# One streaming encoder layer on one core: loads spread over tiles, cached keys turned in head steps, and a reordered SSD

## The chip, the cores and the metric

The kernel runs on one core of a Trainium2 chip. The metric is the device time of one execution in microseconds. Matrix products run on TensorE (PE, with its weight loads shown as PEld), elementwise work on VectorE (DVE), ScalarE (ACT) and GpSimd (POOL); SyncE (SP) and POOL issue most of the DMAs. Products are either fp32, which the trace shows as two instructions each, or fp32r, one instruction each. Where fp32 accuracy is kept with fp32r, a number is split into a high and a low part and the products of the parts are summed.

## What is computed

A layer reads 2048 prompt rows and 64 sample rows of width 1024. The stages after the input projection that matter here, cut from the reference:

```python
# A: attention over the own 64 rows and the 512 before; the sample reads 512 cached keys first
s = einsum('bqhd,bkhd->bhqk', q, concat([k_cache, k_new])) * scale + bias; p = softmax(s); o = p @ v
# B: Mamba-2 SSD in chunks of 128 rows, 6 heads of 64, 2 groups, state 128
acum = cumsum(dt * a)                      # per chunk
decay = exp(where(causal, acum[l] - acum[s], -inf))
y_diag = einsum((c_l . b_s) * decay, x * dt)
st = einsum(b, x * dt * exp(acum[-1] - acum));  h = h * exp(acum[-1]) + st
y = (y_diag + (c . h_prev) * exp(acum) + d_skip * x) * silu(z)
# C: gated MLP, per chunk of 128 and 4 groups:  u * (tril(w) @ v + b)
mixed = concat(rms(o_a), rms(o_b), rms(o_c))
x = layer_norm(alpha * x + mixed @ w_out)
# then up-projection, causal convolution, SwiGLU, down-projection, layer norm
```

Keys of the last 512 prompt rows and of the sample, the final SSD states and convolution states are outputs too.

## The kernel before

Seven stages run one after the other, each a block with a program for every engine and semaphores between them: `project_rows`, `project_features`, `attention`, `ssd_and_gmlp`, `mix_out`, `ffn_up`, `ffn_down`. The order of the work on each engine is written out by hand. Between two stages all engines meet.

`attention` (L916) walks 17 tiles of rows (`Band`), the last being the sample, and in each six heads. One head step on PE (L1238) is `score` of the head after next, `turn` (transposes of the softmax weights, L1214) and `out` of the previous head (L1232). DVE adds the bias (L1091), copies turned blocks (L1119) and normalises (L1106); ACT does the exponential (L1155) and the other turned blocks (L1165). Ahead of tile 14 the loop is left, and `turn_cache` (L1245) turns the 512 cached keys: for each head four transposes into `ps_o` (L1253), a rounded high part by ACT (L1178), the low part by DVE (L1139). Behind the last head, PE turns the keys of five blocks back into rows (L1266, L1267), DVE copies them (L1147), and SP stores them and waits for the stores (L1045). POOL stores the output rows and waits for its stores.

`ssd_and_gmlp` (L1271) begins with DMAs for four constants (`d_row`, `ws`, `gb`, `st_in`, L1350 to L1361), for which PE and POOL wait (`small_loaded`), and with the loads of chunks 0 to 3 (`xbc`, `z`, `uv`, L1355 to L1357). Then 17 chunks run (L1322): 0 to 3 written out, 4 to 11 in a loop, 12 to 16 written out. On PE a step is

```python
front(t + 1)      # 5 transposes into ps_r; 6 fp32 products with `upper` (cumulative sums) into ps_a; 2 products into ps_c
state products into ps_st; products with the state into ps_off; 6 into ps_diag; 4 gate products into ps_c (L1640)
```

On DVE a step copies two small vectors (L1492, L1493), forms the differences of sums from `ps_a` (six operations, L1504), masks `ps_c` (L1508), then `y1` (L1537), the new state (L1539), the mixing matrix of the next chunk (L1518), `y3` (L1545) and the gated output `oc` (four operations, L1551). ACT copies the turned rows (L1446) and takes the exponential (L1448). POOL scales (L1407 to L1409), decays the state (L1416), adds the skip (L1419) and gates with `z` (L1423, `ob`). SP stores `oc` and `ob` and then loads chunk t+4 into the slot of chunk t. Ahead of the loop SP issues the eight loads of `w_out` in one go (L1381) and one of `g_mix`. From chunk 12 on ACT rounds two of the eight `w_out` blocks per step (L1461).

`mix_out` (L1668) walks 17 tiles of rows: 48 products with `w_out` (L119 to L121), transposes of the next tile's `mx` (L1994) and of the last tile's result (L2002), and on DVE scaling, sum and layer norm, of which L1941 writes the result. SP loads `mx` and `x` two tiles ahead (L1753, L1760). Ahead of tile 8 SP also issues, in one go, the loads of the first unit of `ffn_w_in` (L1779) and four blocks of the transposed result (L1783 to L1786), which ACT and DVE prepare for `ffn_up` in tiles 9 to 13.

## Time and profile before

| what | value |
|---|---|
| time, median of 3 runs | 2712.58 us (2704.79 to 2712.89) |
| time of the profiled execution | 2708.32 us |
| its span, first to last instruction | 2706.9 us |
| mean granted TensorE clock | 0.976 |
| PE busy | 2554.4 us, 94% of the span |
| PEld busy | 2349.3 us, 87% |
| DVE busy | 1636.4 us, 60% |
| ACT busy | 1052.8 us, 39% |
| POOL busy | 190.1 us, 7% |
| attention, first to last product | 609 to 839 us |
| SSD and gated MLP | 845 to 983 us |
| mixing | 986 to 1226 us |

A busy share is a mean over stages with different limits. A row of the timeline gives the start in us, the duration in us, the engine, the line, the operation, output and inputs, how many it stands for, and in brackets the idle time of the engine before it with what ended that. SPq is the DMA queue of SP: its rows are issues.

### The profile page before, as it was taken

To read this page: it belongs to the slowest core of one execution; us is meant where nothing else is said; L and a number is where in the kernel's file an instruction comes from. 1 tells how busy PE (TensorE), PEld (TensorE's weight loads), DVE (VectorE), ACT (ScalarE), POOL (GpSimd) and SP (SyncE) were. 2 spreads that over 40 slices of the span, in tenths; PEclk is the share of its full clock that TensorE was granted. 3 is DMA by queue.
4 is the path that set the end of the run, shared out by engine and by line. 5 is a ranking of instruction groups with operands and counts; after the bars stand their busy time and mean duration, and the time that the engine had idled before them with its cause. 6 is when DMAs were issued, how large, how long until landed. Compare 5 with 4: busy or idle time off the path is not lost. (4 is left out here: it accounts for less than half of the span.)

```text
span 2706.9 us, 46923 instructions
## 1 busy us (share of the span) xinstructions
PE 2554.4 (94%) x15072; PEld 2349.3 (87%) x15072; DVE 1636.4 (60%) x3300; ACT 1052.8 (39%) x2000; POOL 190.1 (7%) x276
## 2 busy tenths in 40 slices
PE   6999899989997889897999999999999999999998
PEld 5888799989987878777999989999999978888885
DVE  5433455457775776677999966668666653333332
ACT  4454422226552232225555544445555451111110
POOL 0001100011002641010000000000000000000000
PEclk9999999999998989999999999999999999999999
DMA  6446434236543734548777788887888753223221
GB/s 195 152 139 200 159 108 158 78 102 155 123 98 116 237 131 156 198 140 262 232 253 243 248 286 262 258 256 233 257 256 254 247 187 119 80 80 94 79 79 52
DMA packets 407770, 471.10 MB, mean 174 GB/s; under 512 B 40074, under 2 KB 340732, under 8 KB 407650
## 3 DMA queue, kind: packets, MB, share of 16 engines
q1 hardware_dynamic: 388722, 409.13, 48.4%
q0 software_dynamic: 18944, 60.64, 7.0%
q8 instruction: 58, 0.95, 0.2%
q14 instruction: 46, 0.38, 0.0%
HBM read 315.00 MB, written 157.57 MB: 175 GB/s over the span
## 5 line engine op out<-in xcount | busy, mean ns | idle before, releaser
L2612 PE MATMUL fu_ps_a<-mo_fu_x_hi,mo_fu_w 128*128 128x354 f32 (+1 forms) x1056 | 347.1, 329 | 23.6 <-DVE fu_c L2575 9.6
L2614 PE MATMUL fu_ps_a<-mo_fu_x_hi,mo_fu_w 128*128 128x354 f32 (+1 forms) x1056 | 344.4, 326 | 0.0
L119 PE MATMUL fd_ps_y<-fu_fd_w,fu_fd_h_hi 128*128 128x512 f32 (+1 forms) x748 | 292.4, 391 | 6.7 <-PEq L2043 6.1
L120 PE MATMUL fd_ps_y<-fu_fd_w,fu_fd_h_hi 128*128 128x512 f32 (+1 forms) x748 | 291.7, 390 | 0.0
L121 PE MATMUL fd_ps_y<-fu_fd_w,fu_fd_h_lo 128*128 128x512 f32 (+1 forms) x748 | 291.5, 390 | 0.0
L2803 DVE TENSOR_TENSOR fu_fd_h_lo<-fu_fd_h_raw,fu_fd_h_hi 128x256 fp32r<-128x256 f32 (+1 forms) x185 | 76.9, 416 | 308.9 <-ACT fu_fd_h_hi L2773 308.8
L2613 PE MATMUL fu_ps_a<-fu_x_lo_rest,mo_fu_w 128*128 128x354 f32 (+1 forms) x792 | 257.3, 325 | 0.0
L2773 ACT CAST fu_fd_h_hi<-fu_fd_h_raw 128x256 fp32r<-128x256 f32 (+1 forms) x185 | 74.0, 401 | 403.2 <-PE fd_ps_y L121 396.4
L2612 PEld LDWEIGHTS fu_ps_a<-mo_fu_x_hi,mo_fu_w 128*128 128x128 f32 x1056 | 200.4, 190 | 31.6 <-DVE mo_fu_w L2485 10.9
L2614 PEld LDWEIGHTS fu_ps_a<-mo_fu_x_hi,mo_fu_w 128*128 128x128 f32 x1056 | 200.1, 189 | 0.0
L2612 PE MATMUL fu_ps_c<-mo_fu_x_hi,mo_fu_w 128*128 128x354 f32 (+1 forms) x528 | 173.2, 328 | 8.7 <-ACT fu_part L2407 8.7
L119 PEld LDWEIGHTS fd_ps_y<-fu_fd_w,fu_fd_h_hi 128*128 128x128 f32 (+1 forms) x748 | 138.4, 185 | 40.2 <-issue 6.4
L2613 PE MATMUL fu_ps_c<-fu_x_lo_rest,mo_fu_w 128*128 128x354 f32 (+1 forms) x528 | 172.9, 327 | 0.0
L2614 PE MATMUL fu_ps_c<-mo_fu_x_hi,mo_fu_w 128*128 128x354 f32 (+1 forms) x528 | 172.4, 327 | 0.0
L121 PEld LDWEIGHTS fd_ps_y<-fu_fd_w,fu_fd_h_lo 128*128 128x128 f32 (+1 forms) x748 | 138.4, 185 | 32.0
L120 PEld LDWEIGHTS fd_ps_y<-fu_fd_w,fu_fd_h_hi 128*128 128x128 f32 (+1 forms) x748 | 138.5, 185 | 31.4
L119 PE MATMUL pr_ps_y<-pr_w_hi,pr_xt_hi 128*128 128x512 f32 (+3 forms) x408 | 148.6, 364 | 4.7 <-DVE pr_xt_lo L382 4.7
L2613 PEld LDWEIGHTS fu_ps_a<-fu_x_lo_rest,mo_fu_w 128*128 128x128 f32 x792 | 149.9, 189 | 0.0
L120 PE MATMUL pr_ps_y<-pr_w_lo,pr_xt_hi 128*128 128x512 f32 (+3 forms) x408 | 147.8, 362 | 0.0
L121 PE MATMUL pr_ps_y<-pr_w_hi,pr_xt_lo 128*128 128x512 f32 (+3 forms) x408 | 147.0, 360 | 0.0
L2353 ACT ACTIVATE fu_gate<-fu_c,fu_vecs 128x352 f32<-128x352 f32 (+1 forms) x132 | 90.1, 682 | 85.0 <-DVE fu_c L2556 69.1
L119 PE MATMUL mo_ps_y<-sg_mo_w_hi,sg_mo_mt_hi 128*128 128x512 f32 (+1 forms) x272 | 109.2, 401 | 6.1 <-POOL mo_ident L127 6.1
(396 smaller groups left out, 6239.2 us busy)
## 6 DMA issues: line engine op xcount, KB each, us to landing
mo_fu_w<-fu_w_split SPq DMA_DIRECT2D x176, 512.0 KB, 4.4
fu_w_raw<-ffn_w_in SPq DMA_DIRECT2D x131, 512.0 KB, 5.7
fu_w_split<-mo_fu_w SPq DMA_DIRECT2D x44, 1024.0 KB, 5.9
fu_fd_h_raw<-h_t SPq DMA_DIRECT2D x176, 128.0 KB, 2.2
h_t<-fu_val SPq DMA_DIRECT2D x88, 176.0 KB, 1.9
fu_fd_raw<-ffn_w_out SPq DMA_DIRECT2D x22, 512.0 KB, 4.4
x_rows<-pr_xr SPq DMA_DIRECT2D x16, 512.0 KB, 2.8
xt<-pr_xt SPq DMA_DIRECT2D x16, 512.0 KB, 4.0
```

The source lines that it names most:

```text
L119: pe.matmul(out, lhs_hi, rhs_hi, start=first, stop=False)
L120: pe.matmul(out, lhs_hi, rhs_lo, start=False, stop=False)
L121: return pe.matmul(out, lhs_lo, rhs_hi, start=False, stop=last)
L2353: act.activation(out, src[:, 0:n], ACT.Identity, bias=one(vecs[:, 3, :], mt), scale=one(vecs[:, 0, :], mt)).then_inc(tap0_done, 1)
L2612: pe.matmul(out, wh, xh, start=first and k == 0, stop=False, skip_group_check=True)
L2613: pe.matmul(out, wh, xl, start=False, stop=False, skip_group_check=True)
L2614: last = pe.matmul(out, wl, xh, start=False, stop=k == KH - 1, skip_group_check=True)
L2773: act.copy(h_hi[:, x.slot, :, :x.n], h_raw[:, x.slot, :, :x.n]).then_inc(h_hi_done, 1)
L2803: dve.tensor_tensor(h_lo[:, x.slot, :, :x.n], h_raw[:, x.slot, :, :x.n], h_hi[:, x.slot, :, :x.n].bitcast(F32), ALU.subtract).then_inc(h_l ...
```

## The change

- Attention: two of the four blocks of a head's cached keys are turned in each of the twelve head steps of tiles 14 and 15; four of the five blocks of keys are turned back inside the last two head steps. POOL issues the loads of SSD chunks 0 and 1 at the beginning of tiles 14 and 15 and of the four constants at tile 16. SP and POOL no longer wait for the stores at the end; SP does so at the end of the SSD stage.
- SSD: chunks 0 and 1 are read where attention put them; SP loads 2 to 5 at the beginning. The two small copies move from DVE to ACT, and so do the differences, as `Relu` with a scale of -1 ahead of the exponential. The sums are made from a high and a low part in fp32r. PE does the gate products of chunk t in `front(t + 1)`, behind the sums, and DVE writes `oc` right behind the mask. POOL decays the state first and gates chunk t-1 behind the scaling of t+1. `oc` and `ob` have semaphores of their own. `w_out` is loaded block by block, behind the stores of chunks 0 to 3 and of chunks 4, 6, 8 and 10.
- Mixing: the loads for `ffn_up` are spread over tiles 8 to 12, between the `mx` and the `x` load of a tile, and the work on them moves to tiles 10 to 15.

```diff
 attention, PE and POOL
+                    if turns_cache(b):
+                        turn_cache(b, h)
...
+                def turn_cache(b, h):
+                    i, n = turn_of(b, h), HEADS * b.t + h
+                    if i == 0:
+                        pe.wait_ge(cache_loaded, 16 * 8)
+                    pe.wait_ge(o_done, n - 1)
+                    for k in range(2):
+                        twice = cache[:, 2 * (i % 2) + k, i // 2].rearrange("p a f -> p (a f)")
+                        last = pe.transpose(ps_o[:, i % 2, k * P:(k + 1) * P], twice, ident[:])
...
+                    if turns_cache(b):                       # out()
+                        pe.wait_ge(cache_lo_done, turn_of(b, h) + 1)
...
-                sp.wait_ge(rows_stored, 32)
...
+                pool.wait_ge(next_loaded, 16 * 10)
 SSD, SP
+                for t in range(2, 6):
+                    load(t, t % 4)
...
-                    if not isinstance(t, int) or t + 4 <= NT:
+                    if not isinstance(t, int) or 2 <= t and t + 4 <= NT:
                         load(t + 4, b)
+                    if isinstance(t, int) and t < 4:
+                        sp.dma_start(mo["w_raw"][:, t, :], d["w_out"][t * P:(t + 1) * P, :]).then_inc(mo["w_loaded"], 16)
+                    if not isinstance(t, int) and b % 2 == 0:
+                        k = 2 * i + 2 + b // 2
+                        sp.dma_start(mo["w_raw"][:, bass.ds(k, 1), :], d["w_out"][bass.ds(k * P, P), :]...).then_inc(mo["w_loaded"], 16)
 SSD, POOL
                 def step(t, b, p, i):
+                    decay(t)
                     if not isinstance(t, int) or t + 1 <= NT:
                         scale(t + 1, 1 - p)
-                    back(t, b, p, i)
+                    if not (isinstance(t, int) and t == 0):
+                        gate(t - 1, (b - 1) % 4, 1 - p, i if b else i - 1)
+                    add_own(t, p)
 SSD, ACT
+                    for h in range(HEADS):
+                        last = act.activation(seg[:n, p, h, :n], ps_a[:n, h * P:h * P + n], ACT.Relu, bias=cum_t[:n, p, h:h + 1], scale=-1.0)
+                    last.then_inc(seg_done, 1)
                     act.wait_ge(seg_done, t + 1)
-                    act.activation(seg[:n, p, :, :n], seg[:n, p, :, :n], ACT.Exp).then_inc(exp_done, 1)
+                    act.activation(seg[:n, p, :, :n], seg[:n, p, :, :n], ACT.Exp, scale=-1.0).then_inc(exp_done, 1)
...
                     if 12 <= t < NT:
+                        act.wait_ge(mo["w_loaded"], 16 * KD)
                         for k in (2 * (t - 12), 2 * (t - 12) + 1):
-                            act.wait_ge(mo["w_loaded"][k], 16)
 SSD, PE
                     for h in range(HEADS):
-                        last = pe.matmul(ps_a[:n, h * P:h * P + n], dta_t[:n, p, h:h + 1].to_broadcast([n, n]), upper[:n, :n],
-                                         start=True, stop=True)
+                        for e in range(2):
+                            steps = dta_t[:n, p, e * HEADS + h:e * HEADS + h + 1].to_broadcast([n, n])
+                            last = pe.matmul(ps_a[:n, h * P:h * P + n], steps, upper_r[:n, :n], start=e == 0, stop=e == 1)
                     last.then_inc(cum_done, 1)
                     wait_if(pe, cbm_done, t)
                     wait_if(pe, oc_done, t - 1)
+                    if not (isinstance(t, int) and t == 0):
+                        gates(t - 1, (b - 1) % 4)
 mixing, SP
+                    if isinstance(t, int) and t >= 8:
+                        load_next(t)             # between load_mx(t + 2) and load_x(t + 2)
...
+                    if t == 8:                   # the two halves of unit_raw
+                    if t == 9:                   # X_T1
+                    if t == 10:                  # X_B22
+                    if t == 11:                  # X_B11
+                    if t == 12:                  # X_B21
```

## Rows read from the trace of the kernel before

**Rows 1.** Timeline (columns as told above) of the cached keys' turn, 783 to 791 us.

```profile
783.44 1.06 PE L1253 MATMUL at_ps_o<-at_ident,at_cache 128*128 128x128 f32 x8 [0.67 <-DVE at_o L1106]
...
787.02 0.69 DVE L1139 TENSOR_TENSOR pf_at_k<-at_ps_o,pf_at_k 128x512 fp32r<-128x512 f32 x1 [1.01 <-ACT pf_at_k L1178]
...
790.91 0.49 PE L1199 MATMUL at_ps_s<-pf_at_k,pf_at_q 128*128 128x512 f32 x1 [1.40 <-DVE pf_at_k L1139]
```

**Rows 2.** Timeline from the last head to the first SSD product, 830 to 853 us.

```profile
830.36 0.19 PEld L1266 LDWEIGHTS at_ps_s<-at_ident_r,pf_at_k 128*128 128x128 f32 x1
...
836.64 0.33 PEld L1267 LDWEIGHTS at_ps_s<-at_ident_r,pf_at_k 128*128 128x128 f32 x1
...
840.29 0.52 SPq L1044 DMA_DIRECT2D sample_k<-at_k_rows  x1
844.81 0.21 POOL L125 MEMSET sg_ident<- 128x128 f32 x1 [12.75 <-POOLq L919]
...
853.04 1.09 PE L1588 MATMUL sg_ps_off<-sg_ident,sg_ws 128*128 128x128 f32 x4 [13.79 <-DMA sg_st_in<-state_ssm]
```

**Rows 3.** Timeline of PE's weight loads in one SSD chunk, 867 to 875 us.

```profile
867.70 0.52 PEld L1607 LDWEIGHTS sg_ps_c<-sg_xbc 128*128 128x128 f32 x4 [0.91 <-issue]
...
872.17 1.42 PEld L1601 LDWEIGHTS sg_ps_a<-sg_upper,sg_dta_t 128*128 128x128 f32 x12
...
874.23 0.52 PEld L1607 LDWEIGHTS sg_ps_c<-sg_xbc 128*128 128x128 f32 x4 [0.64 <-issue]
```

**Rows 4.** Busy time by stretch: start:end, length, then each engine, PEclk, DMA share, GB/s.

```profile
880.57:893.60 13.03, 12.11 (x98) 11.79 (x98) 11.63 (x37) 3.07 (x4) 10.08 (x13) 1.00 0.67 195
906.60:919.70 13.10, 8.63 (x56) 8.63 (x57) 5.68 (x18) 1.53 (x2) 5.17 (x6) 0.74 0.81 275
```

**Rows 5.** Timeline of the chunk loads and of w_out's, 866 to 912 us.

```profile
866.89 0.99 POOL L1423 TENSOR_TENSOR sg_ob<-sg_y,sg_z 128x384 f32<-128x384 f32 x1 [1.43 <-DVE sg_y L1545]
...
869.85 0.43 SPq L1357 DMA_DIRECT2D sg_uv<-uv_rows  x1
...
892.59 3.35 SPq L1381 DMA_DIRECT2D sg_mo_w_raw<-w_out  x5
...
911.07 0.93 PEld L1596 LDWEIGHTS sg_ps_r<-sg_ident,sg_xbc 128*128 128x128 f32 x5 [6.58 <-DMA sg_uv<-uv_rows]
```

**Rows 6.** Timeline of the mixing's layer norm on DVE, 1097 to 1164 us, and PE's stall.

```profile
1097.64 1.28 DVE L1941 SCALAR_TENSOR_TENSOR mo_y<-mo_y,mo_rs,mo_b_ln 128x1024 f32<-128x1024 f32 x1
...
1117.17 1.97 PE L1994 MATMUL mo_ps_m<-mo_ident,sg_mo_mx 128*128 128x128 f32 x8 [10.93 <-DVE sg_mo_mx L1890]
...
1135.54 1.29 DVE L1941 SCALAR_TENSOR_TENSOR mo_y<-mo_y,mo_rs,mo_b_ln 128x1024 f32<-128x1024 f32 x1
1148.22 1.28 DVE L1941 SCALAR_TENSOR_TENSOR mo_y<-mo_y,mo_rs,mo_b_ln 128x1024 f32<-128x1024 f32 x1
...
1162.07 1.63 DVE L1974 TENSOR_TENSOR mo_fu_xb<-mo_fu_xb 128x1416 f32<-128x1416 f32 x1
```

**Rows 7.** Timeline of an ordinary head step, 769 us.

```profile
769.30 0.53 PEld L1214 LDWEIGHTS at_ps_t<-at_ident,at_s 128*128 128x128 f32 x5
...
769.74 0.83 DVE L1091 CUSTOM_DVE_ANT_0 at_s<-at_ps_s,pf_bias 128x640 f32<-128x640 f32 x1 [0.41 <-PE at_ps_s L1200]
```

**Rows 8.** DMA issues, 867 to 885 us: count, KB each, us to landing.

```profile
sg_xbc<-xbc_t SPq DMA_DIRECT2D x3, 448.0 KB, 4.3
```

**Rows 9.** Groups by line, 880 to 945 us: busy us, mean ns, idle before, releaser.

```profile
L1504 DVE TENSOR_SCALAR sg_seg<-sg_ps_a,sg_ncum_t 128x128 f32<-128x128 f32 x54 | 14.7, 336 | 5.3 <-PE sg_ps_a L1601 5.3
...
L1448 ACT ACTIVATE sg_seg<-sg_seg 128x768 f32<-128x768 f32 x9 | 7.6, 844 | 26.6 <-DVE sg_seg L1504 26.6
...
L1446 ACT COPY sg_rows<-sg_ps_r 128x640 f32<-128x640 f32 x8 | 5.5, 692 | 24.1 <-PE sg_ps_r L1596 24.1
...
L1461 ACT CAST sg_mo_w_hi<-sg_mo_w_raw 128x1024 fp32r<-128x1024 f32 x2 | 2.0, 1035 | 0.0
```

**Rows 10.** Timeline of ACT in the last chunk: a table load.

```profile
972.06 1.28 ACT L1474 ACT_TABLE_LOAD   x1
```

More of the change, by code:

```diff
@@ L1335, in chunks, with in_place, slot @@
                 step(t, t % 4, t % 2, t // 4)
+        def in_place(t):
+            return isinstance(t, int) and t < 2
+        def slot(name, t, b):
+            if in_place(t):
+                return head[name][:, t]
+            return {"xbc": xbc_slots, "z": z_slots, "uv": uv_slots}[name][:, b]
         def col(t):
@@ L1624, in step @@
                     wait_if(pe, y1_done, t)
[L1625 to L1626 removed]
                     for g in range(2):
                         c = slice(3 * g * HD, 3 * (g + 1) * HD)
[L1629 removed]
+                        last = pe.matmul(ps_off[:n, c], slot("xbc", t, b)[:, 5 + g, :n], state[:, c], start=True, stop=True)
                     last.then_inc(off_done, 1)
```

339 lines of the change are left out of this document (197 added, 142 removed).

## The prediction

> **What bounds the kernel now.** I read the page first, then the busy times by stretch, the waits, the timeline of each place that the diff touches, and the DMA issues. PE is busy for 94% of the span, so a gain must come from a stretch in which PE stands idle or runs at the lower clock. The change touches three stages, 609 to 1226 us, and they hold five such places. (1) Ahead of tile 14 PE turns cached keys alone: its ordinary work stops until 790.91 [rows 1]. (2) From the last head at 830.36 to the first SSD product at 853.04 PE has only keys to turn back and then waits 13.79 us, at the end for the constant `st_in` [rows 2]. (3) In the SSD a chunk takes 6.53 us from one pair of `ps_c` products to the next, and just ahead of them PE's loads stand idle for 0.64 us [rows 3]: these products wait for `oc`, the last thing that DVE does in a step. DVE is busy for 11.63 of 13.03 us, POOL for 10.08, ACT for 3.07 [rows 4]: DVE's order sets the period and ACT is free. (4) `w_out`'s burst at 892.59 delays a chunk's loads, and PE's loads stand idle 6.58 us [rows 5]; the granted clock of that stretch is 0.74 [rows 4]. (5) In the mixing PE stands idle 10.93 us [rows 6] behind the burst of six loads for the next stage. The reader is to see in each group which engine's row ends the idle time in brackets.
>
> **Cached keys.** Removed: PE's turn starts at 783.44 after 0.67 us of idle, and scores resume at 790.91, so 790.91 - 783.44 + 0.67 = 8.1 us. Added: 24 transposes in 12 head steps. Five transposes take 0.53 us in a head step [rows 7], in which PE's loads have next to no idle, so two add 0.21 and the twelve steps 2.5 us. DVE has 0.41 us of idle in a step [rows 7] and gets a subtraction of half the size of L1139's 0.69 us [rows 1], 0.35 to 0.45 us: it fills up, and `out` now waits for it. That may cost up to another 0.2 us a step. I take 0.3 in all, 3.6 us; bounds 2.5 and 5.5. Gain 4.5 us (2.6 to 5.6).
>
> **End of attention.** PE still makes the 60 products behind the keys, 48 of them ahead of the last two `out`; as PE is full there, this moves work and removes none. I take 1.5 us (0 to 2.9). The wait for the stores: SP's last issue ends at 840.81 and the next stage begins at 844.81 [rows 2]; the two ends of a stage without such a wait are not in these rows, so I bound the gain by 0 and 2 us and take 1.3. POOL's new wait is for loads issued tiles earlier; behind it nothing is queued but the end of the stage. The ten loads of 2.3 MB for chunks and constants run beside heads whose own loads are few; I cost them at nothing, and if that cover is gone, a head waits as long as one such load lands, 4.3 us [rows 8].
>
> **Start of the SSD.** PE began 853.04 - 844.81 = 8.2 us into the stage. Afterwards it waits only for POOL's masks, four short operations that start with the one of 0.21 us at 844.81 [rows 2]: some 1.2 us. Gain 7.0 us (6 to 7.3). ACT must first split the steps and round `upper`, six short copies in a chain with DVE; they lie beside PE's nine transposes.
>
> **The chunk's period.** PE's own work is 6.53 - 0.64 = 5.9 us [rows 3]. The twelve fp32 instructions of the sums take 1.42 us [rows 3], 0.12 each; the twelve in fp32r that replace them are bounded, as an estimate, by 0.11 us for a load of 0.19 us that overlaps its neighbour [rows 2] and 0.14: 1.3 to 1.7 us, and I keep 1.4. Now the walk through one step of 5.9 us from PE's first transpose: sums end at 2.1, gates 2.9, `ps_c` pair 3.4, `ps_off` 4.6, `ps_diag` 6.0. ACT: rows at 0.9 for 0.69, six `Relu` (bound by the DVE form's 1.6 us for six below and 0.3 each above) from 2.1 to 3.9, exponential 0.84, small copies 0.4: 3.8 of 5.9 us [rows 9]. DVE loses the differences and copies, 1.6 + 0.6 us of its 5.8 per chunk: mask, `oc`, `y1`, state, mixing, `y3` end at 7.5, long before the next mask at 9.4. POOL has 5.2 us: scaling to 3.9, the gate to 4.9, then it waits for `y1` at 5.3 and ends at 6.4, still ahead of the next rows. So PE becomes the bound at 5.9 us and nothing else has less than half a us of slack. Gain 0.64 x 15 periods = 9.6 us. Bounds: 6.2 us a chunk (5.0 us gained) and 5.75 (11.7).
>
> A rule of the Trainium skill speaks against moving the differences: ScalarE: Activation LUTs, section on rules for kernel authors, sends `relu` to VectorE and not to ScalarE. The row gives DVE 0.34 us for one of 128 columns [rows 9], no run here yet has ACT's; by that rule alone the six would rather cost some tenths more, which matters only where ACT is full.
>
> **The loads.** `w_out` no longer comes in a burst. PE's 6.58 us go, and so does the low clock behind them, at which five transposes took 0.93 us [rows 5] and not 0.53 as in [rows 7], and the rest of a chunk likewise: about 1 us. Together 7.5 us gained (5 to 8). But two new waits come. First, SP loads chunk t+4 behind `ob` of chunk t, which POOL now makes a step later. POOL's gate ends at 867.88 and the last of the three loads is issued by 870.28 [rows 5], and a load lands in 4.3 us [rows 8]: 4.9 + 2.4 + 4.3 = 11.6 in the step's time, and PE wants it at 2 x 5.9 = 11.8. Nearly no slack; a rival below. Second, ACT waits ahead of chunk 12 for all eight blocks of `w_out`, and the last is issued only in SP's step 10, behind `ob` of chunk 10, thus in PE's step 11 at 7.3, landing at 11.6, that is 5.7 in step 12. ACT is there at 4.7 of step 11, and behind its wait stand two roundings of 1.035 us [rows 9], rows, `Relu` and exponential of chunk 13. PE's transposes of chunk 14 need these rows at 8.9 instead of 5.9, its sums the `Relu` at 10.5 instead of 6.5: 4.1 us lost, and one more if the clock falls. I take -5 (-7 to 0). SSD's tail: `oc` and gates earlier, DVE relieved: 1.5 us (0 to 3).
>
> **Mixing.** Two tiles took 1135.54 - 1097.64 = 37.9 us where one takes 1148.22 - 1135.54 = 12.7 [rows 6]: 12.5 us lost to the burst. Spread, a tile carries at most 1 MB more beside its 2 MB in 12.7 us, about 240 GB/s, less than the 275 GB/s of a stretch above [rows 4]. The `mx` load stands ahead of the added one in each tile. DVE gets two block operations of 1.63 us [rows 6] in tiles 13 and 14 each, 3.3 us on about 2.4 of idle: it falls 1.8 us behind, while PE wants its low parts 6 us later, and it has made that good by tile 16. Gain 12.5 us (7 to 12.6).
>
> **Sum.** 4.5 + 1.5 + 1.3 + 7.0 + 9.6 + 7.5 - 5 + 1.5 + 12.5 = 40.4 us. Against the profiled execution, 2708.3 us (span 2706.9), that is 2667.9; the three runs' median is 4.3 us above that execution and their lowest 3.5 below, so I leave the forecast at 2668.
>
> **The rivals.** (A) Chunk loads late: each step's loads land after PE wants them. For: the slack of 0.2 us above, and `w_out` and 0.3 MB of stores in the same queue. Against: `xbc` is issued first of the three, and loads overlap. Each us late costs half a us a period, as a slot's cycle spans two steps; at 1.3 us late the period is back at 6.5 and 9.6 us are gone: 2677. (B) `Relu` and the exponential need different tables: two table loads a chunk, 1.28 us each as the one for the square root behind the last chunk [rows 10]. ACT: 3.8 + 2.6 = 6.4 us, and 8.4 in the four chunks with roundings: 0.5 x 12 + 2.5 x 4 = 16 us, 2684. Against: copies and exponentials alternate here without one [rows 9]. The Trainium skill, ScalarE: Activation LUTs, section on table sets, has `relu` in every set, by which this rival would be void; no row has the pair. (C) The slower one: the clock stays at 1.2 GHz in the SSD, because fp32r sums keep the array less busy than fp32 ones. The place where it fell, 830 to 837 us, is one of pure fp32r with 64 columns [rows 2]; here they are 1.4 of 5.9 us, between fp32 groups at full clock [rows 4]. Price: the lower clock stretches a chunk to some 10.5 us, 4.6 x 16 = 74 us on top: 2742. It decides from nine chunks at the low clock on. (D) ACT's wait for `w_out` costs nothing, since the block lands early or ACT runs behind: 2663. (E) The spreading in the mixing does not do what it says: each of four added loads still holds the next `mx` for some 2 us past its slack, 8 us: 2676.
>
> **How the numbers follow.** Forecast as summed 0.55, A 0.13, B 0.04, C 0.04, D 0.14, E 0.10. All but C are faster by over 0.3% (8 us, about what a measurement of this kernel can tell from no change). The best ends of all bounds together give 2655, the worst without a rival 2690; I take 2656 to 2684, which holds D, A, E and B's middle. Faster 0.94, within 0.3% 0.02, slower 0.04.
>
> **What would show it.** Right: no L1253 alone on PE; head steps in tiles 14 and 15 longer by 0.3 us; PE's first SSD product 1.2 us into the stage; `ps_c` pairs 5.9 us apart with no idle ahead of them; one idle stretch of PE of 3 to 4 us at chunk 13 with ACT's cast ending it on a DMA; mixing tiles 12.7 us apart throughout. Wrong: PE's transposes idle on `sg_uv`, table loads in the SSD, or a granted clock under 0.9 from chunk 2 on.

## The result

The changed kernel takes 2684.32 us (median of four runs, 2679.94 to 2686.66) against 2711.05 us (2704.79 to 2712.89) for the kernel before: ratio 0.9905, interval 0.9888 to 0.9921. It is faster by 26.7 us, where 40.4 were forecast against the profiled execution (43 against this median), and it lies 0.3 us above the range. The two profiled executions differ by less, 2706.9 - 2685.2 = 21.7 us of span, and the places below add up to that.

The page of the changed kernel gives the busy time by engine: PE is busy as long as before, ACT 33 us longer, POOL 15 us longer, and DVE only 16 us less.

```profile
span 2685.2 us, 46989 instructions
PE 2555.4 (95%) x15072; PEld 2352.2 (88%) x15072; DVE 1620.2 (60%) x3171; ACT 1086.0 (40%) x2144; POOL 204.7 (8%) x286
```

**Attention.** These lines are the timeline of a head step in tile 14, which answers to [rows 1] and [rows 7]. The two transposes of cached keys stand behind the turn, ACT and DVE split them within the step, and a step takes 787.05 - 784.51 = 2.54 us, where it took 2.33 before. PE no longer turns cached keys alone.

```profile
784.51 0.73 PE L1262 MATMUL at_ps_t<-at_ident,at_s 128*128 128x128 f32 x5
785.08 0.38 PE L1311 MATMUL at_ps_o<-at_ident,at_cache 128*128 128x128 f32 x2
785.50 0.37 ACT L1224 CAST pf_at_k<-at_ps_o 128x256 fp32r<-128x256 f32 x1
786.97 0.41 DVE L1178 TENSOR_TENSOR pf_at_k<-at_ps_o,pf_at_k 128x256 fp32r<-128x256 f32 x1
787.05 0.74 PE L1262 MATMUL at_ps_t<-at_ident,at_s 128*128 128x128 f32 x5
```

**The end of attention and the start of the SSD.** This is PE's timeline, answering to [rows 2]. The products that turn the keys back begin at 822.39 at full clock (0.28 us each); from 825.32 on they take 0.36 to 0.40 us, and the last heads' own products stand behind them: the 20 products of the last `out` take 2.97 us, where they took 1.80 before. The wait for the next stage is 5.55 us and not 13.79.

```profile
822.39 0.30 PE L1326 MATMUL at_ps_s<-at_ident_r,pf_at_k 128*128 128x64 f32 x1
...
825.21 0.28 PE L1326 MATMUL at_ps_s<-at_ident_r,pf_at_k 128*128 128x64 f32 x1
825.32 0.36 PE L1327 MATMUL at_ps_s<-at_ident_r,pf_at_k 128*128 128x64 f32 x1
825.49 0.40 PE L1326 MATMUL at_ps_s<-at_ident_r,pf_at_k 128*128 128x64 f32 x1
...
830.19 0.79 PE L1262 MATMUL at_ps_t<-at_ident,at_s 64*128 64x64 f32 x5
...
833.61 2.97 PE L1282 MATMUL at_ps_o<-pf_at_v,at_pt 128*64 128x64 f32 x20
...
843.54 1.11 PE L1684 MATMUL sg_ps_off<-sg_ident,at_sg_ws 128*128 128x128 f32 x4 [5.55 <-POOL sg_upper L1479]
```

The busy time by stretch behind that product (columns as in [rows 4]) shows PE busy without a break, while the granted clock stays at 0.50, the 1.2 GHz level, until 859 us.

```profile
845.00:850.00 5.00, 5.00 (x25) 4.81 (x24) 0.81 (x2) 2.45 (x8) 3.19 (x4) 0.50 1.05 323
850.00:855.00 5.00, 5.00 (x24) 5.00 (x24) 1.03 (x2) 3.64 (x11) 2.46 (x3) 0.50 1.09 328
855.00:859.00 4.00, 4.00 (x17) 4.00 (x16) 2.12 (x7) 0.57 (x3) 0.29 (x1) 0.50 0.19 69
859.00:861.00 2.00, 2.00 (x18) 2.00 (x18) 2.00 (x3) 0.33 (x1) 1.81 (x2) 0.87 0.00 0
```

**The chunks.** An undisturbed chunk takes 5.82 us, 6.53 before [rows 3]. The timeline of PE's weight loads shows every idle time of over 0.5 us between the first product and the sums of chunk 16, and what ended it. The first four are waits for chunk loads (one is put down to "issue"; the run with early loads below removes it with the others). The 4.00 us in step 13, ahead of the transposes of chunk 14, are ACT's wait for `w_out`, whose row stands in the second fence beside the issue of the last block: ACT had been idle 8.25 us.

```profile
884.60 0.53 PEld L1703 LDWEIGHTS sg_ps_r<-sg_ident,sg_xbc 128*128 128x128 f32 x5 [1.38 <-DMA sg_uv<-uv_rows]
896.91 0.53 PEld L1703 LDWEIGHTS sg_ps_r<-sg_ident,sg_xbc 128*128 128x128 f32 x5 [0.60 <-DMA sg_uv<-uv_rows]
904.31 0.53 PEld L1703 LDWEIGHTS sg_ps_r<-sg_ident,sg_xbc 128*128 128x128 f32 x5 [1.49 <-issue]
922.49 0.53 PEld L1703 LDWEIGHTS sg_ps_r<-sg_ident,sg_xbc 128*128 128x128 f32 x5 [0.65 <-DMA sg_uv<-uv_rows]
938.26 0.93 PEld L1703 LDWEIGHTS sg_ps_r<-sg_ident,sg_xbc 128*128 128x128 f32 x5 [4.00 <-issue]
939.83 2.63 PEld L1712 LDWEIGHTS sg_ps_a<-sg_upper_r,sg_dta_t 128*128 128x128 f32 x12 [0.63 <-issue]
```

```profile
930.48 0.35 SPq L1454 DMA_DIRECT2D sg_mo_w_raw<-w_out  x1
935.37 1.99 ACT L1575 CAST sg_mo_w_hi<-sg_mo_w_raw 128x1024 fp32r<-128x1024 f32 x2 [8.25 <-DMA sg_mo_w_raw<-w_out]
```

The `uv` load is the last of the three that a chunk needs. The four that PE waited for took 6.0, 4.9, 5.9 and 4.7 us from issue to landing. Here is the first, as the list of DMA issues shows it (count, KB each, us to landing):

```profile
sg_uv<-uv_rows SPq DMA_DIRECT2D x1, 256.0 KB, 6.0
```

**The mixing.** DVE's timeline, answering to [rows 6], has 12.65, 12.84 and 12.48 us from tile to tile where the burst stood.

```profile
1087.07 1.28 DVE L2056 SCALAR_TENSOR_TENSOR mo_y<-mo_y,mo_rs,mo_b_ln 128x1024 f32<-128x1024 f32 x1
1099.72 1.28 DVE L2056 SCALAR_TENSOR_TENSOR mo_y<-mo_y,mo_rs,mo_b_ln 128x1024 f32<-128x1024 f32 x1
1112.56 1.28 DVE L2056 SCALAR_TENSOR_TENSOR mo_y<-mo_y,mo_rs,mo_b_ln 128x1024 f32<-128x1024 f32 x1
1125.04 1.28 DVE L2056 SCALAR_TENSOR_TENSOR mo_y<-mo_y,mo_rs,mo_b_ln 128x1024 f32<-128x1024 f32 x1
```

**Where 21.7 us came from.** The table goes by landmarks in the two timelines: the first score, the turn of the sample's fourth head, the end of the keys, the stage's first product, the sums of chunks 2 and 16, the first and the last layer norm of the mixing. A period is the time from one chunk's sums to the next chunk's.

| place | before, us | changed, us | gain | forecast |
|---|---|---|---|---|
| first score to the fourth head (cached keys) | 216.5 | 211.0 | 5.5 | 4.5 |
| fourth head to the last key | 13.7 | 16.9 | -3.2 | 1.5 |
| last key to the first SSD product | 13.8 | 5.55 | 8.25 | 8.3 |
| first product to the sums of chunk 2 | 12.4 | 16.9 | -4.4 | 0 |
| period, 14 chunks: 6.53 and 5.82 | 91.4 | 81.5 | 9.9 | 9.6 |
| over the period: burst before; late loads and ACT's wait after | 8.2 | 13.8 | -5.6 | 7.5 - 5 |
| sums of chunk 16 to the first layer norm of the mixing | 42.77 | 43.14 | -0.4 | 1.5 |
| first to last layer norm | 215.6 | 201.4 | 14.2 | 12.5 |
| ahead of attention and behind the mixing, untouched code | | | -2.6 | 0 |

The 13.8 us are the sum of what the intervals between the sums have over 5.82: 1.45 + 0.68 + 1.57 + 0.72 = 4.4 for loads, 5.15 for ACT's wait, 4.03 for the chunk behind it at the low clock, 0.2 for the rest. Three places, then, take back most of what was forecast: the keys among the heads, the low clock at the start of the SSD, and the waits inside it. Of the mixing's 14.2 us, 12.4 lie in the two tiles of the burst (37.9 and 25.5 us) and 1.6 in the first tile (13.84 and 12.27 us from the first layer norm to the second). A second profile of the changed kernel has 13.87 us there, so these 1.6 us do not come from the change. The untouched code behind the last layer norm takes 1481 to 1486 us over all profiles, so the last row lies within the spread of code that nobody changed.

### The profile page after: what moved, and what is told of

The parts are those of the page before. It is cut to its first block and busy times, and to the rows that moved or that the text cites. A ratio compares the mean times of both kernels' runs of the same rounds, so it can differ in the third digit from the quotient of the medians.

```text
span 2685.2 us, 46989 instructions
## 1 busy us (share of the span) xinstructions
PE 2555.4 (95%) x15072; PEld 2352.2 (88%) x15072; DVE 1620.2 (60%) x3171; ACT 1086.0 (40%) x2144; POOL 204.7 (8%) x286
```

## The experiments

Each is the changed kernel with one edit, if nothing else is said. Where a kernel was run once, its time is given for orientation only, and the verdict rests on the profile. One profile of the chunks is a weak base as well: the same code took 95.3, 98.4, 97.8 and 102.9 us from the sums of chunk 2 to those of chunk 16 in four profiles (the changed kernel, the keys last, the burst in the mixing, and the changed kernel again).

**Keys behind the last head.**

```diff
                     if nxt2:
                         score(nxt2)
-                    if last_heads:
-                        turn_keys(2 * (h - HEADS + 2))
                     turn(cur)
-                    if last_heads:
-                        turn_keys(2 * (h - HEADS + 2) + 1)
                     if prev:
                         out(prev)
...
                 out((Band(NT), 0, HEADS - 1))
-                turn_keys(4)
+                for b in range(5):
+                    turn_keys(b)
```

> The changed kernel, but all five blocks of keys are turned back behind the last head, as before the change. In the changed kernel PE needs 16.8 us from the turn of the sample's fourth head (821.09 us) to the end of the keys (837.9 us), and the kernel before needed 13.3 us for the same work. My theory: blocks 0 to 3 inside the last two heads bring the clock down early, at 825.3 us, and the last head's own work then runs at 1.2 GHz. It expects 13.3 us here, thus 3.5 us less. Rival: the keys cost the same wherever they stand; it expects 16.5 to 17 us. A second question in the same run: PE's clock stays at 1.2 GHz for 15.7 us of work after the SSD's first product. If that comes from the long low stretch before, it should fall to 4 to 6 us here; if it comes from the SSD's own products, it stays 15 to 16 us.

Measured: 2682.86 us. From the fourth head's turn (820.86) to the last key (833.60) it took 12.7 us, against 16.9 in the changed kernel and 13.7 before. The busy time by stretch shows that the clock holds through all heads and falls at 830.

```profile
826.00:828.00 2.00, 2.00 (x20) 2.00 (x19) 0.81 (x2) 0.00 (x0) 0.57 (x1) 1.00 0.02 5
828.00:830.00 2.00, 2.00 (x19) 2.00 (x19) 0.64 (x2) 0.00 (x0) 0.00 (x0) 0.97 0.21 45
830.00:832.00 2.00, 2.00 (x11) 2.00 (x11) 0.47 (x1) 0.00 (x0) 0.00 (x0) 0.50 0.00 0
```

Over all profiles of this study that stretch took 15.3 to 17.4 us with the keys among the heads (11 profiles) and 12.0 to 14.6 with the keys last (5). The cost of the new place is shown. It is larger than this stretch says: the wait that follows is 4.10 us here and 5.55 in the changed kernel, and it is so in every other profile of either order but the one with wide products; why is not shown. The second question is answered too: the sums of chunk 2 still came 16.89 us after the first product, so the early fall is not what keeps the clock down in the SSD. The whole time hardly fell, as late loads and the low clock behind them made the chunks 3 us longer than in the changed kernel's profile.

**Sums in fp32.**

```diff
-                        for e in range(2):
-                            steps = dta_t[:n, p, e * HEADS + h:e * HEADS + h + 1].to_broadcast([n, n])
-                            last = pe.matmul(ps_a[:n, h * P:h * P + n], steps, upper_r[:n, :n], start=e == 0, stop=e == 1)
+                        last = pe.matmul(ps_a[:n, h * P:h * P + n], dta_t[:n, p, h:h + 1].to_broadcast([n, n]), upper[:n, :n],
+                                         start=True, stop=True)
```

> The changed kernel, but with the twelve instructions of the cumulative sums as six fp32 products again instead of twelve fp32r ones. My theory: the fp32r sums with their broadcast left side hold the clock at 1.2 GHz once it is low, so the clock needs 15.7 us of work to come back at the start of the SSD and 10 us behind the stall at 938 us, where the kernel before needed 4.2 and 4.6 us. It expects 4 to 8 us of low clock at the start here, the sums of chunk 2 at 12 to 14 us after the first product instead of 16.85, and 4 to 5 us less in all with what comes back behind the stall. Rival: the low clock comes from the short idle stretch and the keys before it; then the start stays at 15 to 16 us. Both expect the period of an undisturbed chunk to stay within 0.1 of 5.82 us, since the twelve instructions take 1.42 us either way.

Measured: 2681.02 us. The twelve instructions take 2.69 us for chunk 0 and 1.41 for chunk 1, as the weight loads show; in the changed kernel both took over 2.6. The sums of chunk 2 come at 12.47 us. Behind the stall that ends at 930.63 the clock is back by 936.0, after 5.4 us; in the changed kernel it took from 938.3 to 948, 10 us. The two intervals at that stall are hardly shorter for it, 10.35 and 10.23 us against 10.96 and 9.85, as a second stall lies in the latter. The period stayed 5.82.

```profile
843.19 2.69 PEld L1710 LDWEIGHTS sg_ps_a<-sg_upper,sg_dta_t 128*128 128x128 f32 x12
847.98 1.41 PEld L1710 LDWEIGHTS sg_ps_a<-sg_upper,sg_dta_t 128*128 128x128 f32 x12 [0.44 <-issue]
853.80 1.42 PEld L1710 LDWEIGHTS sg_ps_a<-sg_upper,sg_dta_t 128*128 128x128 f32 x12
```

That second stall is the load of chunk 15, late by 2.43 us, and from the sums of chunk 2 to those of chunk 16 it took 96.1 us, no less than 95.3. Two later runs showed an early return with fp32r, so that this one alone does not settle the cause; see the four timed runs below.

**Two semaphores for `w_out`.**

```diff
                     if isinstance(t, int) and t < 4:
-                        sp.dma_start(mo["w_raw"][:, t, :], d["w_out"][t * P:(t + 1) * P, :]).then_inc(mo["w_loaded"], 16)
+                        sp.dma_start(mo["w_raw"][:, t, :], d["w_out"][t * P:(t + 1) * P, :]).then_inc(mo["w_first"], 16)
...
-                        act.wait_ge(mo["w_loaded"], 16 * KD)
+                        act.wait_ge(mo["w_first"] if t < 14 else mo["w_loaded"], 16 * 4)
```

> The changed kernel, but the first four blocks of w_out signal a semaphore of their own, so that ACT waits ahead of chunks 12 and 13 for these alone, and for the last four ahead of chunk 14. My theory: the wait for all eight blocks costs the 5.15 us of the stall that ends at 938 us and the 4.0 us of low clock behind it, 9.2 us together; it expects chunk intervals of 5.8 to 6.6 us throughout from chunk 2 on and some 9 us less. Rival: ACT is full in the chunks with roundings (two of 1.0 us on top of 3.4 of 5.82 us) and DVE too, so that half of it stays: 4 to 5 us less. A second rival: the other chunk loads collide with the w_out block all the same and the stall moves to the load of chunk 14.

Measured: 2679.07 us. Nothing waits in step 13: the interval to the sums of chunk 14 is 5.83. But the load of chunk 15 is then late, the second rival in part, and with the clock falling it costs 7.59 and 9.27 us for two intervals.

```profile
938.02 0.53 PEld L1703 LDWEIGHTS sg_ps_r<-sg_ident,sg_xbc 128*128 128x128 f32 x5 [1.70 <-DMA sg_uv<-uv_rows]
```

From the sums of chunk 2 to those of chunk 16 it took 89.8 us, 5.5 less than 95.3 and not the 9 expected. That the wait of 4.00 us came from the count is shown by its absence; how much it cost in all is known only within the spread told above.

**Early loads.**

```diff
                     sp.dma_start(d["mixed"][tile_rows(t), 2 * AW:], oc[:n, p, :]).then_inc(oc_stored[p], 16)
+                    if again:
+                        sp.wait_ge(off_done, t + 1)
+                        load(t + 4, b, ("xbc", "uv"))
                     sp.wait_ge(ob_done, t + 1)
...
-                        load(t + 4, b)
+                        load(t + 4, b, ("z",))
```

`z` has semaphores of its own, for which POOL's gate waits.

> The changed kernel, but SP loads xbc and uv of chunk t+4 as soon as the products with the state and oc of chunk t are done, some 5 us earlier; z comes behind ob as before, with a semaphore of its own for which POOL waits and not PE. My theory: PE's four waits for chunk loads (1.38, 0.60, 1.49 and 0.65 us, 4.1 us in all) come from the late issue; it expects none over 0.2 us, and 4 us less. Rival: they come from the bandwidth, since the DMA queues are busy at a share of 0.98 to 1.00 from 884 to 896 us while w_out blocks are in flight; then at least half of the 4.1 us stay, at the same places.

Measured: 2680.07 us, and every interval from chunk 2 to chunk 13 is 5.82 us: no wait for a load is left, so the earlier issue cures the lateness. The busy time by stretch where `w_out` is in flight shows that the queues are as full as in the changed kernel (0.99, 317 GB/s) and move more, so a full queue by itself did not make a load late.

```profile
884.00:896.00 12.00, 12.00 (x103) 12.00 (x103) 9.98 (x22) 6.87 (x21) 11.83 (x13) 1.00 1.04 346
```

What is left is ACT's wait, with 2.24 us of idle ahead of chunk 14 and intervals of 9.20 and 9.10. That the queue's load played no part is not shown: of the four late `uv` loads of the changed kernel each landed 0.4 to 1.7 us later than the 4.3 us that the prediction took, about as much as PE waited.

**Differences on DVE again.** The six operations stand ahead of DVE's mask:

```diff
 ACT
-                        last = act.activation(seg[:n, p, h, :n], ps_a[:n, h * P:h * P + n], ACT.Relu, bias=cum_t[:n, p, h:h + 1], scale=-1.0)
 DVE
+                        last = dve.tensor_scalar(seg[:n, p, h, :n], ps_a[:n, h * P:h * P + n], cum_t[:n, p, h:h + 1], 0.0,
+                                                 ALU.subtract, ALU.min)
```

> The changed kernel, but the six differences per chunk are formed on DVE again (subtraction and minimum with zero) ahead of the mask, and ACT takes only the exponential; the new place of oc and of the gate products stays. In the changed kernel DVE is busy for 4.99 of a 6.0 us stretch, its mixing operations lengthened to 1.15 us each from 0.73. My theory: with 1.6 to 2.0 us more DVE has some 6.6 us per chunk and sets the period again, so undisturbed chunks take 6.3 to 6.7 us in place of 5.82, and the run is 7 to 12 us slower than the changed kernel. Rival: the period fell because oc and the gate products moved, and DVE's work has slack; then it stays at 5.82 to 5.95 us.

Measured: 2681.76 us and 5.82 us a chunk: the rival was right for the differences. DVE has no idle time at all (the third busy figure below), and PE still none. The two small copies, some 0.6 us a chunk on DVE before, stayed on ACT in this run; as DVE is full, it does not show that they could go back as well.

```profile
866.00:872.00 6.00, 6.00 (x53) 6.00 (x53) 6.00 (x16) 1.91 (x5) 5.57 (x7) 1.00 0.56 149
```

**The burst in the mixing.** The conditions for tiles 9 to 12 go, so that all six loads are issued at tile 8.

```diff
+                    if isinstance(t, int) and t == 8:
+                        load_next(t)
                     if exists(t, 2):
                         load_mx(t + 2, p)
-                    if isinstance(t, int) and t >= 8:
-                        load_next(t)
...
-                    if t == 9:
...
-                    if t == 10:
```

> The changed kernel, but the six loads for the next stage stand in one go at tile 8 of the mixing, ahead of its mx load, as before the change; the work on them stays in tiles 10 to 15. My theory: the burst alone makes the 12.5 us lost in two tiles before; it expects the layer norms of tiles 8 to 10 to be 24 and 13.7 us apart again, and the mixing 12 to 13 us longer than the 201.4 us of the changed kernel. Rival: part of the gain of 14.2 us is the later work on DVE and ACT; then it is 6 to 10 us longer only.

Measured: 2699.6 us, and DVE's timeline shows the gap of before, with 25.07 and 14.96 us for two tiles.

```profile
1086.56 1.28 DVE L2052 SCALAR_TENSOR_TENSOR mo_y<-mo_y,mo_rs,mo_b_ln 128x1024 f32<-128x1024 f32 x1
1111.63 1.29 DVE L2052 SCALAR_TENSOR_TENSOR mo_y<-mo_y,mo_rs,mo_b_ln 128x1024 f32<-128x1024 f32 x1
1126.59 1.28 DVE L2052 SCALAR_TENSOR_TENSOR mo_y<-mo_y,mo_rs,mo_b_ln 128x1024 f32<-128x1024 f32 x1
```

From the first to the last layer norm it took 216.0 us against 201.4, 14.6 more and not the 12 to 13 expected. The spread loads are thus all of the gain, and the later work on DVE and ACT gave none.

**All four edits at once.** These are the first four diffs together.

> The changed kernel with four edits at once: keys turned back behind the last head, sums in fp32, two semaphores for the blocks of w_out, and the early loads of xbc and uv. My theory: the stall ahead of chunk 13 and the four waits for loads go (13.8 us over the 81.5 us of 14 undisturbed periods), the end of attention gives 4.2 us and the start of the SSD 4.4 us, so the sums of the last chunk come 94 to 97 us after the first product in place of 112.2, and the time is 2662 us (2657 to 2667), 0.982 of the kernel before. Rival: with the stalls gone the w_out blocks and the chunk loads collide in chunks 13 to 15, where the split of w_out and two more loads of mx stand; then 5 us of it stay, 2667 to 2671 us.

Measured: 2658.9 us (2658.03 to 2660.07), ratio 0.9816 (0.9802 to 0.9829). From the sums of chunk 2 on all intervals are 5.82 us, but for the last with 5.91; the sums of chunk 16 come 94.04 us after the first product, where 94 to 97 were expected, and the time is within its 2657 to 2667 too. PE's weight loads show no idle time over 0.2 us between chunk 1 and chunk 16.

```profile
842.40 1.41 PEld L1711 LDWEIGHTS sg_ps_a<-sg_upper,sg_dta_t 128*128 128x128 f32 x12 [0.74 <-issue]
929.89 0.77 PEld L1711 LDWEIGHTS sg_ps_a<-sg_upper,sg_dta_t 64*64 64x64 f32 x12 [0.20 <-issue]
```

**Wide products in the gap.** They come on top of the four edits:

```diff
+                for k in range(5):
+                    pe.matmul(ps_t[:, 512:1024], keys(0, 0, 12), kr[:, 12, 0:512], start=True, stop=True)
...
+                for k in range(2):
+                    pe.matmul(ps_diag[:, 0:256], ws[:, 0, :], ws[:, 0:2, :].rearrange("p g j -> p (g j)"), start=True, stop=True)
```

> The kernel with the four edits, and in the gap between the two stages PE does five wide fp32r products of 512 columns behind the keys and two fp32 products of 256 columns ahead of the wait for the masks; nobody reads them. My theory: they are PE work in a gap, so the clock, low from 829.9 us on in the run with the keys last, comes back by the first chunk's sums instead of some 4 to 6 us after the first product; 1.5 to 2 us less up to the sums of chunk 2. Rival: five products at the low clock take 2.1 us and the clock counts from the stage's start all the same, since there is still an idle wait of 2 us between; no gain, or up to 1 us lost.

Measured: 2662.01 us. The clock was back for the first sums (1.42 us for twelve), but from the last key to the sums of chunk 2 it took 15.84 us, against 16.0 to 16.6 in the three runs with the keys last and an early return. That is 0.1 us below the lowest of them, where 1.5 to 2 us less were expected, so no gain is shown.

**`oc` last.** It stands behind `y3` again.

```diff
                         causal(t + 1, 1 - p)
-                    dve.wait_ge(gm_done, t + 1)
-                    for g in range(CG):
...
                     dve.tensor_tensor(y3[:n, :], y2[:n, :], ps_diag[:n, 0:AW], ALU.add).then_inc(y3_done, 1)
+                    dve.wait_ge(gm_done, t + 1)
+                    for g in range(CG):
```

> The changed kernel, but DVE writes oc behind y3, as the last thing of its step, as before the change; the differences stay on ACT and the gate products stay in PE's next step. The run with the differences back on DVE kept the period of 5.82 us, with DVE busy for 6.00 of 6.00 us, so the move to ACT is not what shortened it. Theory: it was the place of oc. With oc last, PE's products into ps_c wait for it again: but DVE has 1.66 us less in its step here, so oc ends at about 8.4 us counted from PE's first transpose and is wanted at 8.7; it expects a period of 5.82 to 6.0 us. Rival: either edit alone is enough, as each takes 1 to 2 us out of the time from the sums to oc; it expects 5.82 exactly.

Measured: 2707.62 us, a period of 7.45, and both expectations are far off. PE's weight loads stand idle ahead of the gate products in every step, from the third on for 1.0 to 1.9 us.

```profile
868.06 0.97 PEld L1692 LDWEIGHTS sg_ps_c<-sg_uv,sg_wt 128*128 128x128 f32 x8 [1.55 <-issue]
```

`oc` ran at 867.09 to 867.94, behind `y3` and the two mixing operations, which took 2.22 us together. I had DVE's walk end at 8.4 us with mixing operations of 0.73 us.

**Both undone.** This is the last diff and that of the differences together.

> The changed kernel with both edits undone at once: the differences on DVE and oc behind y3 (the gate products stay in PE's next step, POOL's order stays). If the new place of oc or the move to ACT, either one, gave the period, it is back at 6.4 to 6.8 us here and PE's loads stand idle ahead of the products into ps_c. If it was neither, but the gate products or POOL's new order, it stays at 5.82 to 5.9 us.

Measured: 2708.6 us, with intervals of 7.2 to 7.5 us and 9.1 to 9.3 in several; 6.4 to 6.8 were expected. The differences add nothing here either. In the changed order the place of `oc` decides between 7.45 and 5.82 us a chunk. That is more than the gain of 0.71 over the kernel before, so the rest of the new order costs time while `oc` is last; what the gate products, POOL's order and the moved copies give by themselves was not separated.

**`w_out` in one go again.** The loads block by block go, and the eight stand ahead of chunk 4.

```diff
-                    if isinstance(t, int) and t < 4:
-                        sp.dma_start(mo["w_raw"][:, t, :], d["w_out"][t * P:(t + 1) * P, :]).then_inc(mo["w_loaded"], 16)
...
                     if t == 4:
+                        for k in range(KD):
+                            sp.dma_start(mo["w_raw"][:, k, :], d["w_out"][k * P:(k + 1) * P, :]).then_inc(mo["w_loaded"], 16)
```

> The changed kernel, but the eight loads of w_out come in one go ahead of chunk 4, as before the change, with the one semaphore for which ACT waits ahead of chunk 12. Theory: the burst stalls PE for 6 to 8 us once, with 5 to 10 us of low clock behind it, since the sums are fp32r; in return the stall of 5.15 us ahead of chunk 13, its 4.0 us of low clock and the waits for single loads behind chunk 7 go. It expects the sums of the last chunk 110 to 115 us after the first product against 112.2 in the changed kernel: the spreading gave nothing net as it was done. Rival: the spreading is worth its 7.5 us, the burst costs more than the late wait, and the chunks take 117 us or more.

Measured: 2687.66 us. The burst cost 10.26 us of idle and a chunk at the low clock, two intervals of 16.62 and 10.33; behind it the intervals were 5.82 or 5.83, 6.06 and 6.88. The sums of chunk 16 came 110.9 us after the first product, inside the theory's 110 to 115. But the start was quick here (chunk 2's sums at 12.29), so I compare from there: 98.6 us to chunk 16, against 95.3 in the one profile of the changed kernel and 102.9 in the other. That the spreading as it was done is worth anything net is not shown.

```profile
899.57 0.93 PEld L1699 LDWEIGHTS sg_ps_r<-sg_ident,sg_xbc 128*128 128x128 f32 x5 [10.26 <-DMA sg_uv<-uv_rows]
900.49 2.68 PEld L1708 LDWEIGHTS sg_ps_a<-sg_upper_r,sg_dta_t 128*128 128x128 f32 x12
```

**Four timed runs on one chip.** They are the changed kernel, the same with fp32 sums, with the other three edits, and with all four.

> The changed kernel itself, as the base for the next three on the same chip. Expected 2680 to 2687 us, and a profile in which the sums of chunk 2 come 16 to 17 us after the stage's first product, or, where the clock returns early as it did in one run of nine, 12.3 us.

> The changed kernel with fp32 sums, timed. If the type of the sums delays the clock's return, the median is 3 to 6 us below that of the changed kernel on the same chip, and the sums of chunk 2 come 12.3 to 12.5 us after the first product again. If the three early returns were chance, the medians agree within 1.5 us and the profile may show either.

> The kernel with three of the four edits (keys last, two semaphores, early loads), the sums left in fp32r. If the sums cost what they seem to, it is 3 to 6 us above the kernel with all four, thus 2662 to 2665 us, with 16 to 17 us from the first product to the sums of chunk 2. If not, it is at 2658 to 2660 us like the kernel with all four.

> The kernel with all four edits again, on the same chip as the three before. Expected 2657 to 2661 us and the sums of chunk 2 12.3 to 12.6 us after the first product; any other interval there would speak against the sums as the cause.

| kernel | median, us | lowest to highest | ratio to before (interval) | sums of chunk 2 after the first product |
|---|---|---|---|---|
| changed | 2685.44 | 2679.86 to 2692.27 | 0.9903 (0.9885 to 0.9922) | 16.74 us |
| fp32 sums | 2679.94 | 2678.55 to 2680.45 | 0.9885 (0.9867 to 0.9903) | 12.48 |
| three edits, fp32r sums | 2659.97 | 2658.92 to 2661.33 | 0.9813 (0.9798 to 0.9829) | 11.86 |
| four edits, fp32 sums | 2660.08 | 2657.11 to 2660.68 | 0.9812 (0.9797 to 0.9827) | 12.17 |

In the changed kernel the median is 5.5 us lower with fp32 sums, though the lowest of its runs, 2679.86 us, lies within theirs, and their spread is 1.9 us against 12.4. Beside the other three edits they give nothing: the run with three edits met the expectation for sums that do not cost (2658 to 2660 us), and the early sums of chunk 2 in the last run, 12.17 us, lie outside the 12.3 to 12.6 that I had tied to the sums as the cause. The profiled run of the changed kernel, its slowest with 2692.27 us, shows what the spread is made of: a load late by 2.55 us, and the chunk behind it takes 894.66 - 885.55 = 9.11 us and not 5.82, since the clock fell.

```profile
885.06 0.53 PEld L1703 LDWEIGHTS sg_ps_r<-sg_ident,sg_xbc 128*128 128x128 f32 x5 [2.55 <-DMA sg_uv<-uv_rows]
885.55 2.28 PEld L1712 LDWEIGHTS sg_ps_a<-sg_upper_r,sg_dta_t 128*128 128x128 f32 x12
894.66 1.42 PEld L1712 LDWEIGHTS sg_ps_a<-sg_upper_r,sg_dta_t 128*128 128x128 f32 x12
```

With fp32 sums a late load, of 1.68 us, made intervals of 8.09 and 6.87. At the start of the SSD the clock came back late in 9 of 11 profiles with fp32r sums (chunk 2's sums at 15.2 to 16.9 us) and early in 2 (12.29 and 11.86), and early in 5 of 5 with fp32 sums (the kernel before counted, the run with wide products not). So the sums' type goes with the delay but does not fix it alone: with fp32r sums and the keys last, the sums of chunk 2 came at 16.89 us in one kernel and at 11.86 in another whose PE code up to there is the same. Why those two came back early stays open, and with it what delays the clock in the others.

## Why the prediction was wrong

The sign and six of the nine terms held in size: cached keys (4.5 forecast, 5.5 measured), the start of the SSD with the wait for stores (8.3 and 8.25), the period (9.6 and 9.9), the burst (7.5 and 8.2), the mixing (12.5 and 14.2, of which 12.4 in the tiles of the burst). The gain stayed out in the places that follow.

- **End of attention: forecast +1.5, measured -3.2.** The failed step is "mixed with fp32 work the fall may come later or not at all". I priced the low clock for the keys alone. It fell about as far into the keys, 3.0 us against 3.2 before, and as the keys now stand ahead of the last heads' work, that work ran at 1.2 GHz too. The run with the keys last gives it back.
- **Start of the SSD: forecast 0, measured -4.4.** The failed step is a missing term: I took the gap as the whole cost and did not ask at which clock the stage starts. Rival C came nearest, fp32r sums that hold the clock down, but it had them lower the clock for the whole stage, at 74 us. In undisturbed chunks the clock is full with either kind of sums; the delay shows where it is already low, at the start. That fp32r sums cause it is not shown, as two of eleven profiles with them had none.
- **ACT's wait: forecast 5, measured 9.2** (5.15 and 4.03). The place and the cause were right, the idle of PE too, "3 to 4 us" against 4.00. Mis-sized was the clock, "one more if the clock falls": 9.2 less the 4.1 of the wait leaves 5 us, because the clock took 10 us to return, more than a chunk and a half.
- **Late chunk loads: forecast 0, with rival A at 0.13.** The walk gave 0.2 us of slack, and four loads were late, 4.4 us with what follows, more in the run of 2692.27 us. The failed step is "a load lands in 4.3 us", a row of `xbc` ahead of `w_out`'s burst: the last load of a chunk is `uv`, and the four late ones took 4.7 to 6.0 us. The early loads show that an issue ahead of `ob` gives slack enough for that.
- **Tail of the SSD: forecast +1.5, measured -0.4.** From the sums of chunk 16 to the first layer norm of the mixing it took 42.8 us before and 43.1 in the changed kernel, so the term "`oc` and gates earlier, DVE relieved" gave nothing. No run looked into it, and the cause stays open.
- **The period was right in part by luck.** The step "DVE loses the differences" has no part in it: with the differences back the period is the same. It is `oc` ahead of the state work, worth 1.6 us in the new order. The durations were wrong as well: a mixing operation takes 1.15 us and not 0.73, and POOL's decay 1.15 and not 0.83, as the groups of the changed kernel show.

```profile
L1619 DVE TENSOR_TENSOR sg_mix<-sg_seg,sg_cbm 128x384 f32<-128x384 f32 x20 | 22.2, 1147 | 0.0
L1498 POOL TENSOR_TENSOR sg_decayed<-sg_state,dt_etot 128x384 f32<-128x384 f32 x10 | 11.5, 1146 | 0.0
```

The Trainium skill, GPSIMD Engine Reference, section on specifications, says that the engine shares its SBUF interfaces with VectorE, with contention for DVE instructions that have two SBUF inputs. These mixing operations have two, and the rows agree. They show more: the two engines take turns. In the timeline of the changed kernel a mixing operation ends 0.41 us after the POOL operation that it started beside (872.52 and 872.11; 873.63 and 873.21), and POOL's decay, started in between, ends 0.69 us after the mixing operation. The kernel before has the same 0.41 us (872.41 and 872.00); where POOL was idle, a mixing operation took 0.55 us.

```profile
871.11 1.00 POOL L1511 TENSOR_TENSOR sg_y<-sg_y,sg_xd 128x384 f32<-128x384 f32 x1
871.41 1.11 DVE L1619 TENSOR_TENSOR sg_mix<-sg_seg,sg_cbm 128x384 f32<-128x384 f32 x1
872.07 1.14 POOL L1498 TENSOR_TENSOR sg_decayed<-sg_state,dt_etot 128x384 f32<-128x384 f32 x1
872.45 1.18 DVE L1619 TENSOR_TENSOR sg_mix<-sg_seg,sg_cbm 128x384 f32<-128x384 f32 x1
...
865.81 0.55 DVE L1518 TENSOR_TENSOR sg_mix<-sg_seg,sg_cbm 128x384 f32<-128x384 f32 x1
871.54 0.87 DVE L1518 TENSOR_TENSOR sg_mix<-sg_seg,sg_cbm 128x384 f32<-128x384 f32 x1
```

The last two lines are from the kernel before. All mixing operations together took 23.8 us before and 37.3 in the changed kernel. That is one reason why moving 2.2 us a chunk away lowered DVE's busy time by so little, and it made the expectation for `oc` last fail.

Rival B is void: the only table load of the stage stands at 961.68 us, in the last chunk as before [rows 10]. Six `Relu` take 1.66 us on ACT, as many differences 1.63 on DVE. The rule on `relu` of the Trainium skill, ScalarE: Activation LUTs, section on rules for kernel authors, is thus neither confirmed nor costly here: at 128 columns of fp32 both engines need about 0.28 us each. Rival D fell, and so did E: where the loads are spread, the tiles of the mixing are 12.5 to 12.8 us apart.

The range missed by 0.3 us for the median and by 1.4 us for that of the later five runs. Its upper end held the cases one by one, but late loads, the clock at the start, the cost of the keys and a longer wait came together. That it missed by so little is luck: the profiled executions differ by 21.7 us, not 26.7, and the mixing and the cached keys gave 2.7 us more than forecast.

## What to carry to other kernels

Price a stall together with the clock behind it: here 2 to 4 us of idle cost 3 to 5 us more at 1.2 GHz, while the waits of 0.6 to 1.5 us in the changed kernel left the clock at 1.00 and cost little more than themselves. A load with 0.2 us of slack is thus worth moving even where it looks just in time. Take the landing time from the row of the load that comes last, and from a stretch with the same traffic. Don't put a run of narrow products ahead of real work, but behind the last of it. When loads are counted on one semaphore, ask at which count each waiter could go on; and when an order changes, find by undoing one move at a time which of the moves pays, since here `oc` ahead of the state work decided the period and moving the differences off DVE gave nothing. Compare profiles of the same code before you read 3 us out of one profile.

## What the runs showed of the hardware

- In the changed kernel PE was busy without a break at a granted clock of 0.50 for 15.5 us, from 843.5 to 859 us. Being busy did not bring the clock back in that time. The products there were fp32 transposes and products with fp32r sums between them. In all 17 profiles of this study the clock came back at the latest 16.1 us after the stage's first product.
- The clock fell while PE was busy throughout, in all 17 profiles within 2.1 to 5.0 us of the first of the products that turn the keys back, which are fp32r with 64 columns: after 3.2 us in the kernel before, 3.0 in the changed one, 4.2 in the run with the keys last. The Trainium skill, TensorE: Matmul & The Clock Gate, section on what's actually happening, has activity release the throttle and idleness bring it back; these rows show a clock that falls, and in the item above one that stays low, with PE never idle.
- Twelve fp32r products, six sums as pairs of a high and a low part, take the same 1.42 us as six fp32 products in two instructions each; at the low clock both take 2.6 to 2.7 us.
- A DVE operation with two SBUF inputs that takes 0.55 us alone takes 1.11 to 1.18 us beside POOL operations, and a POOL operation of 0.83 us beside it up to 1.15: each ends a fixed 0.41 or 0.69 us after the other engine's operation.
